# The gates of the RG-LRU as split products: three single-pass matmuls in place of one in plain 32 bits

## The reference, cut to what matters

```python
xr = dwconv(xr, conv_w, LRU_PAD) + conv_b            # the same for the 256 context tokens
def rglru_coeffs(xc, w_r, b_r, w_i, b_i, lam):
    xb = xc.reshape(bsz, s, LRU_BLOCKS, LRU_BLOCK)   # 8 blocks of 64 channels
    r = sigmoid(einsum("bsgi,gij->bsgj", xb, w_r).reshape(bsz, s, LRU_WIDTH) + b_r)
    i = sigmoid(einsum("bsgi,gij->bsgj", xb, w_i).reshape(bsz, s, LRU_WIDTH) + b_i)
    log_a = -LRU_C * r * softplus(-lam)
    return exp(log_a), sqrt(-expm1(2.0 * log_a)) * (i * xc)
```

## Time and profile before

| | us |
|---|---|
| median of three runs (2540.52 to 2541.5) | 2540.53 |
| the profiled execution, its own time | 2539.45 |
| its span, first to last instruction | 2537.3 |
| TensorE busy | 2451.8 (97% of the span) |

### The profile page before, as it was taken

The page is one execution under the profiler, slowest core; times in us unless marked ns, Lnnn a source line. Parts: engine busy times, 40 slices in busy tenths (PEclk is TensorE's granted clock), DMA queues, the critical chain, the costliest instruction groups (busy, mean ns, idle before and its releaser), DMA issues.

```text
span 2537.3 us, 29607 instructions
## 1 busy us (share of the span) xinstructions
PE 2451.8 (97%) x11210; PEld 1999.0 (79%) x11210; DVE 1127.9 (44%) x1460; ACT 524.7 (21%) x805; POOL 1068.2 (42%) x511
## 2 busy tenths in 40 slices
PE   7899999989899999999999899999799999999999
PEld 3687777778788888888888688887688888888887
DVE  4666647864844434422223634245622222222224
ACT  3334437861200000000001200002200000000003
POOL 2133336799544444333444234442533333433440
PEclk9999999999999999999999999999899999999999
DMA  9543356533333332311111011111111111111111
GB/s 286 150 136 129 129 155 140 92 107 106 100 117 116 100 109 96 109 50 50 50 50 51 17 50 50 41 53 39 50 49 43 50 49 42 50 50 50 50 33 67
DMA packets 223198, 206.55 MB, mean 81 GB/s; under 512 B 40119, under 2 KB 193427, under 8 KB 222611
## 3 DMA queue, kind: packets, MB, share of 16 engines
q1 hardware_dynamic: 216643, 186.64, 25.6%
q10 hardware_dynamic: 5904, 16.78, 1.8%
q0 software_dynamic: 576, 2.10, 0.2%
HBM read 185.20 MB, written 20.28 MB: 81 GB/s over the span
## 4 chain that ended last, share of the span: by engine, by line
PE 88%; DVE 4%; POOL 3%; issue 2%; ACT 1%; DMA 0%; POOLq 0%; DVEq 0%; SPq 0%; ACTq 0%
PE bank L727 27%; PE bank L729 27%; PE bank L728 27%; PE bank L852 1%; DVE sumsq L1323 1%; PE bank L810 1%; DVE probs L1570 1%; POOL k_lo L628 1%; PE bank L759 1%; PE bank L895 1%; DVE act_lo L1350 1%; ACT probs L1215 1%; POOL q_st L630 1%; DVE h L1367 1%; POOL act_lo L656 1%
## 5 line engine op out<-in xcount | busy, mean ns | idle before, releaser
L574 POOL TENSOR_TENSOR w_hi<-raw,ones 128x1024 fp32r<-128x1024 f32 x200 | 393.2, 1966 | 1214.5 <-PE bank L729 1167.0
L727 PE MATMUL bank<-act_hi,w_hi 128*128 128x512 f32 x2176 | 855.2, 393 | 10.4 <-DVE act_lo L1350 4.5
L728 PE MATMUL bank<-act_hi,w_lo 128*128 128x512 f32 x2176 | 851.6, 391 | 0.0
L729 PE MATMUL bank<-act_lo,w_hi 128*128 128x512 f32 x2176 | 851.5, 391 | 0.0
L577 POOL TENSOR_TENSOR w_lo<-raw,w_hi 128x1024 fp32r<-128x1024 f32 x200 | 510.1, 2551 | 15.7
L727 PEld LDWEIGHTS bank<-act_hi,w_hi 128*128 128x128 f32 x2176 | 411.5, 189 | 101.4 <-issue 6.3
L729 PEld LDWEIGHTS bank<-act_lo,w_hi 128*128 128x128 f32 x2176 | 411.4, 189 | 86.7
L728 PEld LDWEIGHTS bank<-act_hi,w_lo 128*128 128x128 f32 x2176 | 411.5, 189 | 84.6
L1367 DVE SCALAR_TENSOR_TENSOR h<-bank,mods,h 128x512 f32<-128x512 f32 x432 | 319.8, 748 | 216.4 <-PE bank L729 215.1
L1610 DVE TENSOR_TENSOR hid_f<-silu_g,bank 128x512 f32<-128x512 f32 x88 | 60.6, 689 | 706.2 <-PE bank L729 704.9
L727 PE MATMUL bank<-hid_hi,w_hi 128*128 128x512 f32 x704 | 276.6, 393 | 3.5 <-DVE h L1367 3.5
(11 more groups left out here) (187 smaller groups left out, 2330.2 us busy)
## 6 DMA issues: line engine op xcount, KB each, us to landing
raw<-in_ffn_w_gu SPq DMA_DIRECT2D x88, 512.0 KB, 3.9
mod_in_f<-in_mod_w SPq DMA_DIRECT2D x48, 512.0 KB, 4.7
raw<-in_ffn_w_down SPq DMA_DIRECT2D x44, 512.0 KB, 3.6
mod_in_p<-in_mod_w SPq DMA_DIRECT2D x32, 512.0 KB, 6.7
raw<-in_o_w_in SPq DMA_DIRECT2D x24, 512.0 KB, 3.7
raw<-in_e_w_in SPq DMA_DIRECT2D x20, 512.0 KB, 5.0
mod_ring<-in_mod_w SPq DMA_DIRECT2D x16, 512.0 KB, 4.8
raw<-in_e_w_out SPq DMA_DIRECT2D x16, 512.0 KB, 4.0
```

The source lines that it names most:

```text
L574: nc.gpsimd.tensor_tensor(w_hi, raw[:, parity, :], ones[:, 0:1].to_broadcast([P, UNIT]), ALU.mult).then_inc(s_hi, 1)
L727: pe.matmul(dst, w_hi, x_hi, start=first, stop=False)
L728: pe.matmul(dst, w_lo, x_hi, start=False, stop=False)
L729: return pe.matmul(dst, w_hi, x_lo, start=False, stop=last)
```

## The change

The operands of the gate products are divided into high and low parts, and each product becomes a call of `product`. ACT copies `gate_w` and `x_conv` into the rounded high parts `gate_hi` and `xc_hi`, DVE subtracts to get the low parts `gate_lo` and `xc_lo`. The new tiles lie over storage that is free at that time: `xc_lo` over `x_pad`, `xc_hi` over the second half of `lru_q`. The chunks of columns are cut as 256, 512, 512 instead of 512, 512, 256. TensorE waits for the low parts where it waited for `x_conv` and for the loaded `gate_w`; ACT makes the high parts between the groups 7 and 8, with a wait for the load of `gate_w`, one for `x_conv`, and in i = 0 one for earlier stores. DVE makes the low parts after `mod_set`, in i = 0 after `convolve(0)`.

```diff
+        GATE_CHUNKS = ((0, CTX, 2), (CTX, HALF, CTX + 5), (CTX + HALF, HALF, CTX + 5 + HALF))
             def gates(i):
-                pe.wait_ge(s_conv, i + 2)
-                pe.wait_ge(s_gw, i * 128 + 128)
+                pe.wait_ge(s_gwl, i + 1)
+                pe.wait_ge(s_xcl, i + 1)
                 if i:
                     pe.wait_ge(s_mset, i)
                 for g in range(12):
-                    lo = (g % 3) * HALF
-                    w = min(HALF, KEYS - lo)
+                    lo, w, low = GATE_CHUNKS[g % 3]
                     pe.wait_ge(s_gatev, 12 * i + g + 1)
-                    pe.matmul(bank[:, 5 + g % 3, 0:w], gate_w[:, g // 3, :], x_conv[:, lo:lo + w],
-                              start=True, stop=True).then_inc(s_gate, 1)
+                    product(bank[:, 5 + g % 3, 0:w], (gate_hi[:, g // 3, :], gate_lo[:, g // 3, :]), xc_hi[:, lo:lo + w],
+                            xc_lo[:, low:low + w], True, True).then_inc(s_gate, 1)
...
                     act.dma_start(dst, qk_out[:, o, 0:w]).then_inc(s_qk, 16)
+                if i == 0:
+                    act.wait_ge(s_filled, 64)
+                act.wait_ge(s_gw, i * 128 + 128)
+                nc.scalar.copy(gate_hi[:], gate_w[:]).then_inc(s_gwh, 1)
+                act.wait_ge(s_conv, i + 2)
+                nc.scalar.copy(xc_hi[:], x_conv[:]).then_inc(s_xch, 1)
                 act.wait_ge(s_lru, i + 1)
...
+            def gate_low(i):
+
+                dve.wait_ge(s_gwh, i + 1)
+                V.tensor_tensor(gate_lo[:], gate_w[:], gate_hi[:], ALU.subtract).then_inc(s_gwl, 1)
+                dve.wait_ge(s_xch, i + 1)
+                V.tensor_tensor(xc_lo[:, 2:2 + CTX], x_conv[:, 0:CTX], xc_hi[:, 0:CTX], ALU.subtract)
+                V.tensor_tensor(xc_lo[:, CTX + 5:CTX + 5 + SEQ], x_conv[:, CTX:], xc_hi[:, CTX:], ALU.subtract).then_inc(s_xcl, 1)
+
             dve.wait_ge(s_pad, 3)
             convolve(0)
+            gate_low(0)
             for i in range(LT):
                 recur(i)
                 if i + 1 < LT:
                     convolve(i + 1)
                 mod_set(i, i + 2)
+                if i + 1 < LT:
+                    gate_low(i + 1)
```

More of the change, by code:

```diff
@@ L180, in backbone @@
         x_pad = at(68, "x_pad", [P, KEYS + 6])
+        xc_lo = at(68, "xc_lo", [P, KEYS + 6], F32R)
+        xc_hi = at(25, "xc_hi", [P, KEYS], F32R)
+        gate_hi = at(96, "gate_hi", [P, 4, P], F32R)
+        gate_lo = at(66, "gate_lo", [P, 4, P], F32R)
         x_conv = at(73.5, "x_conv", [P, KEYS])
@@ L236, in backbone @@
         s_gate, s_gatev = sem("gate_done"), sem("gate_evacuated")
+        s_gwh, s_gwl, s_xch, s_xcl = sem("gate_w_hi"), sem("gate_w_lo"), sem("x_conv_hi"), sem("x_conv_lo")
         s_s, s_rs, s_lru = sem("decay_ready"), sem("root_ready"), sem("lru_done")
@@ L1181, in _ @@
                 for g in range(12):
-                    m, lo = g // 3, (g % 3) * HALF
-                    w, of = min(HALF, KEYS - lo), i + (m % 2 * 8 + m // 2 * LT)
+                    m, (lo, w, _) = g // 3, GATE_CHUNKS[g % 3]
+                    of = i + (m % 2 * 8 + m // 2 * LT)
                     act.wait_ge(s_gate, 12 * i + g + 1)
```

## The result

| | before | after |
|---|---|---|
| median of 18 runs each | 2540.47 us (2535.09 to 2541.89) | 2546.27 us (2543.36 to 2551.76) |
| ratio after to before, 95% interval | | 1.0027 (1.0019 to 1.0034) |
| profiled execution, its span | 2539.45, 2537.3 | 2544.41, 2542.3 |
| mean granted clock | 0.988 | 0.984 |

What follows compares the result with a forecast made beforehand. TensorE, 97% busy, was taken to bound the kernel. Four gate stages each 1.68 us shorter, all else costing nothing, made 2540.53 - 6.7 = 2533.8 us, range 2532.2 to 2537.6.

Steps and rivals of the forecast that it cites:

- The price of a stage: Gate stages on TensorE: 6.86 us instead of 8.59; with slip 1.68 us gained a stage, 6.7 in all.
- The two bounds for the loop between TensorE and ACT: Three gates per loop: 1.73 us fits, stage 6.86 us; with the slower weight load 1.84, stage 7.22.
- The new work of ACT: Copies gate_hi and xc_hi, 0.6 and 1.27 us: cost nothing, cover 1.1 us and then 3.5.
- The new work of DVE: Making gate_lo and xc_lo: ready at 185.9 or, doubled, 187.5; cost nothing, cover 3.3 to 4.9 us.
- rival 3: DVE's low parts late at the first gate of three layers; 0.2% slower needs 3.9 us each; chance 0.04.
- Both sides of this race start from the end of the gates before, so the gain doesn't eat the cover: DVE's low parts against TensorE's next gates: both move with the earlier gates, so 3.3 to 4.9 us of cover stays.
- Does the gain reach the end?: After the last stage, at values and scores: 6.5 us left at the values, following program 6.7 us earlier.
- about 1 us either way: Where TensorE idles the granted clock falls; its effect on the following work was bounded at about 1 us.
- The sum: Profiled 2539.45 - 4 × 1.68 = 2532.7 us; median 2540.53 - 6.7 = 2533.8 us.
- the range: Median time 2532.2 to 2537.6 us, from a gain of 8.3 (no slip, kinder clock) to 2.9.
- Rival 2: After the gates, a load, store's landing or lower clock gives gain back: gain 1 to 5, 2537 us; chance 0.17.
- wrong altogether: Signs: a gate stage keeping 8.6 us, or short stages with a new wait beginning the values or attention.

Runs made afterwards that it cites:

- e8_pool_lag: The changed kernel with one small POOL memset delaying the weight split that falls beside DVE's four modulation steps; 2534.38 us, ratio to before 0.9978.
- e1_totals_late: The changed kernel with mod_totals after group 7 instead of group 6, 2.8 us later on TensorE; 2533.55 us, ratio to before 0.9977.
- e3_narrow_last: The changed kernel with the 256-column chunk last in each gate instead of first; 2545.71 us, ratio to before 1.0026.
- e4_before_dve_lag: The kernel before with one added DVE operation of 0.17 us ahead of the four modulation steps; 2551.67 us, ratio to before 1.0050.
- e5_filler: The changed kernel with nine unused 512-column products ahead of the wait at mod_totals; 2540.44 us, ratio to before 1.0001.

## Why the prediction was wrong, step by step

**The price of a stage: right, a little too hopeful.** Forecast 36 matmuls and 6.91 us, measured 36 and 7.03. The two bounds for the loop between TensorE and ACT were 6.86 and 7.22. What holds is seen in the weight loads of the stage of i = 0:

```profile
131.77 0.19 PEld L734 LDWEIGHTS bank<-xc_hi,gate_hi 128*128 128x128 f32 x1 [0.17 <-ACT lru_r L1197]
133.52 0.19 PEld L734 LDWEIGHTS bank<-xc_hi,gate_hi 128*128 128x128 f32 x1 [0.16 <-ACT lru_i L1197]
135.27 0.19 PEld L734 LDWEIGHTS bank<-xc_hi,gate_hi 128*128 128x128 f32 x1 [0.15 <-ACT lru_r L1197]
```

They wait for ACT once a round, and a round is 1.75 us: the sum of its three tanhs, which I had at 1.74 and then took for no limit of its own. ACT runs its twelve tanhs without a gap, from 129.77 to 136.98. 4 × 1.75 = 7.00. So ACT paces the stage, and the term was mis-sized by 0.12 us, 0.5 in all.

**The new work of ACT: right.** `gate_hi` took 0.62 and `xc_hi` 1.26 us, as priced. For i = 1 the forecast cover of 1.1 us shows as 0.96 us of idle time behind `xc_hi` in `e8_pool_lag`, where nothing delays TensorE. (The idle time of 5.14 us in the earlier trace rows counts from 180.29; from 180.64 it is 4.8. Nothing hung on it.) The copies in i = 0:

```profile
119.23 0.62 ACT L1184 CAST gate_hi<-gate_w 128x512 fp32r<-128x512 f32 x1 [0.45 <-ACT qk_out L1175]
119.76 1.26 ACT L1186 CAST xc_hi<-x_conv 128x1280 fp32r<-128x1280 f32 x1
```

**The new work of DVE: no wait, as forecast, so rival 3 is not what happened; but the cover is not always what was forecast.** The narrow subtraction was blocked by POOL as feared, the wide one was not:

```profile
182.66 2.49 DVE L1552 TENSOR_TENSOR xc_lo<-x_conv,xc_hi 128x256 fp32r<-128x256 f32 x1
185.07 1.21 DVE L1553 TENSOR_TENSOR xc_lo<-x_conv,xc_hi 128x1024 fp32r<-128x1024 f32 x1
```

Ready at 186.28, and TensorE wants it at 190.75: 4.5 us of cover, where 3.3 to 4.9 were forecast. But here TensorE comes 3.6 us late itself, so this is no test of the forecast. In `e8_pool_lag`, where DVE's steps take 10.28 and nothing delays TensorE, the cover is 2.9, 4.7 and 4.6 us in i = 1, 2 and 3, at first a little under the forecast. In `e1_totals_late`, with the slow steps and TensorE on time, it is 188.86 - 187.48 = 1.4 us, then 1.4 and 0.9:

```profile
186.27 1.21 DVE L1553 TENSOR_TENSOR xc_lo<-x_conv,xc_hi 128x1024 fp32r<-128x1024 f32 x1
```

```profile
188.86 0.28 PE L734 MATMUL bank<-xc_hi,gate_hi 128*128 128x256 f32 x1
```

So the cure that moves the wait leaves the next wait of TensorE for DVE less than 1 us of cover in i = 3. Rival 3 had the right sign, and the right resource, DVE against POOL. Its place (the first gate), its price (3.9 us of lateness before it decides) and so its chance of 0.04 were wrong.

**The step that failed is "Both sides of this race start from the end of the gates before, so the gain doesn't eat the cover", and with it "Does the gain reach the end?".** The sentence speaks of `xc_lo` and was taken as if it held for every meeting of TensorE and DVE in the layer. I then looked for waits only behind the last stage, at the values and the scores. Between two stages stands `mod_totals`, told of in the description of the kernel and in no step of the prediction, and both sides of its wait were in the trace: the four steps end at 164.46 + 10.29 = 174.75, and TensorE's weight load for the totals is

```profile
174.86 1.31 PEld L759 LDWEIGHTS bank<-ones,mod_acc_p 128*128 128x128 f32 x10
```

0.11 us later. The page shows no wait there, because none was long enough to show. Counted from the end of the gates TensorE comes to the totals as it did before (175.08 - 139.57 = 35.51 us, with the end at 130.98 + 8.59; now 171.61 - 136.09 = 35.52), so the gain alone would not have eaten even the 0.11. What did was the second thing that the prediction never asked: who starts first. DVE's steps and POOL's split both start from the end of the same stage, DVE by way of ACT's coefficients and the recurrence, POOL by way of TensorE's group 4. ACT's first coefficient, right behind its last gate tanh, begins at 140.43 in before and at 137.01 in after:

```profile
140.43 2.81 ACT L1192 ACTIVATE lru_q<-lru_r,sp 128x1280 f32<-128x1280 f32 x2
```

```profile
137.01 2.81 ACT L1204 ACTIVATE lru_q<-lru_r,sp 128x1280 f32<-128x1280 f32 x2
```

From there DVE's first step is 24.03 us away in both kernels. POOL's is 24.08 away in before and 24.03 in after; the other two layers give the same to 0.02 us. ACT paces the shorter stage, so its work ends about 0.06 us later behind TensorE's than it did (0.92 against 0.86), and a lead of 0.05 us was all that DVE had. That the lost lead comes from ACT's pace is the reading of these rows and not shown by a run of its own: `e3_narrow_last` tried to move ACT's end and did not. That the order, however it came about, makes the loss is shown, in both directions (`e4_before_dve_lag`, `e8_pool_lag`). Where the prediction had no wait, the runs show three of 2.04 us each at `mod_totals`, and about 1.5 us at the lower clock behind each.

I had the rule for this in hand. The Trainium skill ("SBUF — State Buffer", on the shared port pair) says that whichever of the two engines starts first gets the pair for the whole instruction. I used it for the two new subtractions and not for the old steps, whose own row I had quoted as proof of it. The traces agree with the rule: with DVE first, a first step of 1.28 us and a first split of 2.98; with POOL first, 2.97 and 1.90; and a memset that puts POOL's split 0.15 us behind DVE's step brings the first case back.

**The clock: "about 1 us either way" was too small.** I took it from how little three executions of before differ, 1 us; the 18 beside the result spread over 6.8 us. And such a spread measures the gaps that exist, not one that is new. In the trace of after the clock behind the new gaps costs 1.5 us each, 4.6 of the 10.8 us that the waits cost in all; in one layer of `e3_narrow_last` and two of `e4_before_dve_lag` it cost about 3.2.

**The sum, put right:** the stages -6.2 instead of -6.7; the waits, +6.1, and the clock behind them, +4.6, where the sum had nothing. -6.2 + 10.8 = +4.6, against +4.7 in the stretch and +5.8 by the medians. The remaining 1 us stays open: the trace is of one execution, 2544.41 us and among the fastest of the 18, and others may have lost more to the clock; no run shows that. A slip in the range decided nothing: no slip and a kinder clock, 6.9 and 1, make a gain of 7.9 and not 8.3. Rival 2, something after the gates that hangs on another clock, was near in kind, but it was allowed to take back at most the gain. The signs that I had named for "wrong altogether" included short stages with a new wait at the values or attention. It was this case, in a third place.

## What to carry to other kernels

Before counting a gain on the busiest engine, list every semaphore that it waits for in the stretch whose timing moves, those that cost nothing now most of all, and write beside each how much earlier the other side is: one with 0.1 us of cover can turn either way, and the page doesn't show it. Where VectorE and GpSimd start large operations at nearly the same moment, ask who is first and by how much; if a wait hangs on it, move the consumer or order the two engines by a semaphore, rather than leave it to hundredths of a microsecond. And when a change loses where it should win, try first to move the wait: `e1_totals_late` changes one digit and turns +5.8 us into -6.3. Then look at the covers again: here the next one was down to 0.9 us.

## What the runs showed of the hardware

- VectorE and GpSimd take turns: with VectorE ahead by 0.05 us at the start four steps took 10.29 us, with GpSimd ahead by 0.01 us 12.46, and alone they took 5.46.
- TensorE's clock: a gap of 2.04 us with 1.8 us of one-column matmuls behind it was followed by 24 products in 4.44 us instead of 2.91, in a window of 5 us at a granted clock of 0.66, that is partly at the level of 1.2 GHz instead of 2.4. The same gap and matmuls were followed by 0.50 in the first layer of `e3_narrow_last` and 0.57 in the second of `e4_before_dve_lag`, so the price of one gap varied, from 1.5 to 3.2 us. The same one-column matmuls kept 1.00 where full products ran up to them, in before and, with nine fillers, in `e5_filler`. So products with an unused result kept TensorE at its higher level and saved 1.6 us each time.
- A plain 32-bit product cost four clocks a column (8.59 us for 5120 columns); three split ones, each with a new weight matrix, 0.235 us per 512 columns and 0.12 per 256 (314.44 to 314.67 to 314.91, and 314.08 to 314.20, in the stage of i = 3), here with a stage of 7.03 us since ACT paced it.
